# Low halves of the routed tokens: made by GpSimd from SBUF instead of by VectorE from PSUM

## What is computed

```python
x = x + hierarchical_moe(rms_norm(x, ffn_norm[l]), ...)      # 4 groups x 8 experts, top 2 of one group
# inside, per token:
pg = softmax(xt @ w_rg + b_rg);  g_w, g_idx = top_k(pg, 1)
le = (xt @ w_re + b_re)[g_idx];  tv, tj = top_k(le, 2)
w_top = softmax(tv) * g_w
# tokens are gathered for each expert, then
gu = xb @ w_e1[e];  ys = (silu(gu[:, :512]) * gu[:, 512:]) @ w_e2[e]
y[token] += ys * w_top
```

## Time and profile before

| | us |
|---|---|
| median of 3 runs | 1590.48 (1589.98 to 1591.97) |
| the profiled execution | 1589.14 |
| its span, first to last instruction | 1587.3 |

### The profile page before, as it was taken

One profiled execution on the slowest core, in us unless ns is written; L12 is line 12 of the kernel. 1 busy time (PEld: TensorE's weight loads), 2 busy tenths in 40 slices (PEclk: granted clock), 3 DMA queues, 4 the chain that ended last, 5 costly groups with the idle time before them and its releaser, 6 DMA issues.

```text
span 1587.3 us, 31259 instructions
## 1 busy us (share of the span) xinstructions
PE 1314.4 (83%) x13623; PEld 1020.7 (64%) x13623; DVE 598.0 (38%) x987; ACT 447.4 (28%) x665; POOL 0.4 (0%) x5
## 2 busy tenths in 40 slices
PE   9999999998777586877679999999986656767755
PEld 8999999995354263544448999999754323324422
DVE  5869647644121101212118885566431101101101
ACT  7544545532120110102016454554301001000101
POOL 0000000000000000000000000000000000000000
PEclk9999999999889788999979999999999988878988
DMA  9843458449999999999997544664799999999996
GB/s 356 294 162 107 160 188 315 147 169 392 416 427 420 427 426 422 427 420 426 427 387 233 198 149 160 242 251 148 281 417 429 425 428 424 427 428 414 427 427 281
DMA packets 93839, 520.02 MB, mean 328 GB/s; under 512 B 9850, under 2 KB 17410, under 8 KB 68356
## 3 DMA queue, kind: packets, MB, share of 16 engines
q1 hardware_dynamic: 92956, 515.94, 81.1%
q10 hardware_dynamic: 744, 2.05, 0.4%
HBM read 515.87 MB, written 2.10 MB: 326 GB/s over the span
## 4 chain that ended last, share of the span: by engine, by line
PE 53%; DMA 36%; DVE 6%; ACT 2%; issue 2%; SPq 2%; DVEq 0%; ACTq 0%
DMA ring<-in_w_expert_out 29%; PE banks L1759 29%; PE banks L2202 6%; PE banks L2155 5%; DMA ring<-in_w_expert_in 4%; PE banks L1790 4%; PE banks L2216 2%; DMA ring<-in_w_in 2%; PE banks L2172 2%; DVE w_lo L1066 1%; DVE stat L1520 1%; PE banks L1988 1%; SPq L514 1%; ACT w_hi L647 1%; DMA lnt<-in_positions 1%
## 5 line engine op out<-in xcount | busy, mean ns | idle before, releaser
L2155 PE MATMUL banks<-ring,arena 128*32 128x256 f32 x3904 | 267.1, 423 | 123.0 <-DMA ring<-in_w_expert_in 117.3
L2155 PEld LDWEIGHTS banks<-ring,arena 128*32 128x32 f32 x3904 | 125.9, 119 | 247.3 <-DMA ring<-in_w_expert_in 147.4
L1066 DVE TENSOR_TENSOR w_lo<-ring,w_hi 128x2048 fp32r<-128x2048 f32 (+1 forms) x103 | 210.5, 2044 | 108.9 <-ACTq L624 97.1
L1759 PE MATMUL banks<-h_hi,w_hi 128*128 128x256 f32 x776 | 221.8, 286 | 0.9 <-DVEq L1057 0.9
L2202 PE MATMUL banks<-ring,arena 128*32 128x256 f32 x2048 | 154.2, 451 | 81.8 <-DMA ring<-in_w_expert_out 68.6
L1759 PE MATMUL banks<-h_hi,w_lo 128*128 128x256 f32 x776 | 219.5, 283 | 0.0
L1002 ACT ACTIVATE arena<-banks 128x128 f32<-128x128 f32 x66 | 18.4, 278 | 689.1 <-PE banks L2155 689.1
L1513 DVE TENSOR_TENSOR arena<-arena,banks 128x128 f32<-128x128 f32 x66 | 19.1, 289 | 504.2 <-ACT arena L1002 504.2
L1759 PE MATMUL banks<-h_lo,w_hi 128*128 128x256 f32 x712 | 201.4, 283 | 0.0
L647 ACT CAST w_hi<-ring 128x2048 fp32r<-128x2048 f32 (+1 forms) x103 | 176.1, 1709 | 70.0 <-PE banks L1759 43.0
L2202 PEld LDWEIGHTS banks<-ring,arena 128*32 128x32 f32 x2048 | 76.2, 125 | 137.4 <-issue 79.4
(11 more groups left out here) (434 smaller groups left out, 2179.9 us busy)
## 6 DMA issues: line engine op xcount, KB each, us to landing
ring<-in_w_expert_in SPq DMA_DIRECT2D x120, 2048.0 KB, 23.3
ring<-in_w_expert_out SPq DMA_DIRECT2D x60, 2048.0 KB, 24.1
ring<-in_w_in SPq DMA_DIRECT2D x23, 2048.0 KB, 9.2
ring<-in_w_branch SPq DMA_DIRECT2D x12, 1024.0 KB, 5.2
ring<-in_w_out SPq DMA_DIRECT2D x4, 2048.0 KB, 7.9
ring<-in_w_xq SPq DMA_DIRECT2D x4, 2048.0 KB, 7.9
ring<-in_w_xo SPq DMA_DIRECT2D x4, 2048.0 KB, 8.4
arena<-in_w_xkv SPq DMA_DIRECT2D x4, 2048.0 KB, 21.3
```

Of the source, the lines that this page charges most:

```text
L1066: post(dve.tensor_tensor(piece_view(w_lo, *key), piece_view(ring, *key), high_view(*key).bitcast(F32), ALU.subtract), "w_split")
L1759: ins = pe.matmul(acc, stationary(a, k), moving(b, k), start=k == 0 and n == 0, stop=k == kc - 1 and n == 2)
L2155: ins = pe.matmul(G[32 * j:32 * j + 32, :], tokens, w[:, k % 4, :, j * P:(j + 1) * P], start=k == 0, stop=k == KC - 1, tile_position=(0, 3 ...
```

## The change

ScalarE now does two instructions for each job j, not one, from the same bank with the same scale: `htok_hi` rounded, and `htok_full` in plain f32. They no longer wait for completion one by one; ScalarE waits once for all eight and then frees the four banks itself. GpSimd, in a queue of its own, waits for both of job j (`htok_high` counts eight per layer) and subtracts, four instructions of 128x512 per layer, both operands in SBUF. `htok_full` is `region(0, TB, D)`, the words 0 to 2047 of `arena`, so the subtraction works in place: `htok_lo` lies over the same words. `token_low` goes from VectorE, with the wait for its end and the freeing of the banks. TensorE's steps r = 0 and 1 wait for two of GpSimd's four subtractions, r = 2 and 3 for all four.

```diff
+        htok_full = region(0, TB, D)
...
         def _(pool):
             pool.memset(ones[:, :], 1.0).then_inc(S["pool_step"], 1)
+            for layer in range(L):
+                for j in range(4):
+                    half, tb = j // 2, j % 2
+                    part = lambda v: v[:, tb, half * 512:half * 512 + 512]
+                    pool.wait_ge(S["htok_high"], 8 * layer + 2 * j + 2)
+                    pool.tensor_tensor(part(htok_lo), part(htok_full), part(htok_hi).bitcast(F32), ALU.subtract).then_inc(S["htok_ready"], 1)
...
                     acc = job_wait(act, layer, "htok", j)
-                    post(act.activation(htok_hi[:, tb, half * 512:half * 512 + 512].rearrange("t (k p) -> t k p", k=4),
-                                        acc.rearrange("t (p k) -> t k p", k=4), ACT.Copy, scale=rstd_tok[:, tb:tb + 1]), "htok_high")
+                    for v in (htok_hi, htok_full):
+                        act.activation(v[:, tb, half * 512:half * 512 + 512].rearrange("t (k p) -> t k p", k=4),
+                                       acc.rearrange("t (p k) -> t k p", k=4), ACT.Copy, scale=rstd_tok[:, tb:tb + 1]).then_inc(S["htok_high"], 1)
+                act.wait_ge(S["htok_high"], 8 * (layer + 1))
+                for j in range(4):
+                    act.sem_inc(free(layer, "htok", j), 1)
...
-                def token_low(r):
-
-                    half, pair = r // 2, r % 2
-                    part = lambda v, tb: v[:, tb, r * T:(r + 1) * T].rearrange("t (k p) -> t k p", k=2)
-                    for tb in range(TB):
-                        dve.wait_ge(S["htok_high"], 4 * layer + 2 * half + tb + 1)
-                        acc = job_wait(dve, layer, "htok", 2 * half + tb).rearrange("t (p k) -> t k p", k=4)
-                        dve.scalar_tensor_tensor(part(htok_lo, tb), acc[:, 2 * pair:2 * pair + 2, :], rstd_tok[:, tb:tb + 1],
-                                                 part(htok_hi, tb).bitcast(F32), ALU.mult, ALU.subtract).then_inc(S["htok_ready"], 1)
...
                 def weights():
-                    for r in range(4):
-                        token_low(r)
-                    dve.wait_ge(S["htok_ready"], 8 * (layer + 1))
-                    for j in range(4):
-                        dve.sem_inc(free(layer, "htok", j), 1)
                     dve.sem_inc(free(layer, "place"), 1)
...
                         if small_jobs:
-                            pe.wait_ge(S["htok_ready"], 8 * layer + 2 * r + 2)
+                            pe.wait_ge(S["htok_ready"], 4 * layer + 2 * (r // 2) + 2)
```

## The result

The changed kernel took 1603.52 us (median of 6 runs, 1599.37 to 1604.37) against 1590.23 us before (6 runs, 1589.56 to 1591.97): ratio 1.0077, 95% interval 1.0067 to 1.0088, so it is 0.8% slower, 12 to 13 us. The forecast was 1602.8 us, slower. The profiled execution took 1599.37 us, the lowest of the six (the next is 1602.38), with a span of 1597.2 us; what it shows is about 4 us less than what the median has.

The account below looks back on a forecast made before the run. TensorE held 53% of the chain that ended last, DMA 36%; delay before the gather's release counts in full. Per layer -0.17 + 4.12 + 2.2 = 6.15 us, twice 12.3, made the median 1602.8 us; range 1590 to 1607.

Parts of the forecast that it names:

- Where the stage stands: Stretch from TensorE's filling to the experts' first ring load: every microsecond of delay before the gather's release counts in full.
- VectorE: Per layer, removing token_low's eight instructions (3.22 us) saves only TensorE's wait for its first pair: -0.17 us.
- ScalarE: Eight instructions per layer, 0.63 us apart, finish before the first gather is done: 0 us, with 0.3 kept as possible.
- GpSimd's own time: Four 128x512 subtractions per layer at 1.2 us each, ending at 361.5 if undisturbed, in time for TensorE.
- limit of 3.3 us for one subtraction: Up to this length per GpSimd subtraction, TensorE's wait for the new low halves was to cost nothing.
- rival of a late GpSimd: GpSimd starts late or one subtraction takes over 3.3 us: +6 to +10 us per layer, 1602 to 1610; chance 0.06.
- The hold: GpSimd's subtractions delay VectorE's serial router chain by full exclusion: mask 4.12 us late per layer, at 364.47.
- The rule: Two-SBUF-input VectorE instructions and SBUF-reading GpSimd instructions share one read interface; the second waits for the whole first: 4.12 us.
- The clock: After 5.0 us idle before `place`, TensorE runs at half clock: 2.2 us per layer, ends 0 and 2.5.
- The sum: Per layer -0.17 + 4.12 + 2.2 = 6.15 us, twice 12.3, giving a median of 1602.8 us.
- rival of no disturbance: VectorE's chain keeps its 0.25 us steps while GpSimd subtracts: 1590.1 us, or 1590.7 with ScalarE's 0.3; chance 0.22.
- the one with the clock up: GpSimd's subtractions delay VectorE's chain but TensorE's clock holds: +7.9 us, 1598.4 us; chance 0.19.

## Why the prediction was right

- *Where the stage stands.* The delay in front of the first ring load went to the end in full, but for 1.45 us of 11.35 (the 0.25, 0.25 and 0.95 of above), which are no larger than the runs of one kernel differ.
- *VectorE*: put at -0.17 us. The wait for `htok_lo` is gone, and in the run with more filling, where the clock stays up, the gather starts 369.34 - 367.01 = 2.33 us after `place`, not 2.85; at the ring load 0.39 us of this is left. So the term was too small by 0.2 us. Freeing 3.2 us of VectorE gave no more than that.
- *ScalarE*: free, as put. Eight instructions every 0.57 us, where 0.63 was taken.
- *GpSimd's own time*: 1.23 us for a subtraction, where 1.2 was taken from VectorE's row of twice the columns. That it came so near is in part luck: GpSimd's only row, 0.205 us for 128 columns, would make 2.5 us for three passes over 512 columns, not 1.0 to 1.4. The Trainium skill's figure (GPSIMD Engine Reference, § Performance versus the Vector engine), scaled, gave an estimate of 1.12, a tenth too low here. The subtractions were ready in time (361.1, needed at 363 and later). The forecast's limit of 3.3 us for one subtraction holds for the first two only; all four by 366.5 from 356.5 on allows 2.5 us. At 1.23 us neither mattered, and the rival of a late GpSimd is out.
- *The hold*: 4.12 us in the sum, 3.70 measured. The step was right and its walk off in one place: I let the TENSOR_SCALAR L1462 (L1473 after) pass as a one-operand instruction. It was held, 1.20 us, and one two-operand instruction fewer instead. What made the sum smaller is when the row of subtractions ended: 361.13, not 361.93, because ScalarE delivered faster and GpSimd went from one to the next without letting VectorE in between; the instruction held behind one subtraction ended within 0.1 us of its end, when the next had begun. In these traces VectorE gets one such instruction for each subtraction, and a hold for each: four for four, two for two.
- *The rule*: the Trainium skill (SBUF — State Buffer, § Who interferes with whom) has this, and the runs agree: GpSimd's reading holds VectorE's two-operand instructions (copies, subtractions), its writing alone does not (memsets), reductions pass in 0.22 us, and TENSOR_SCALAR is named there as one that can take the shared pair in a two-port mode, which is the sentence I had not applied (1.20 us beside a subtraction, and the lengthened 0.23 us beside a memset would fit it too). The runs show one direction only. That GpSimd waits for VectorE in turn was in my walk, but no trace here shows it: all subtractions from two tiles took 1262 to 1281 ns.
- *The clock*: 2.2 us per layer in the sum, with an end of 2.5. Measured 2 to 3 by the times, with 3.2 (2.1 to 4.3) where it is measured by itself, and 2.7 in that run's trace. The end of 2.5 was too low: the changed kernel's layer 0 lost 3.07 us, with the clock at half from before 364 to past 370, six to seven us and not 4.9.
- *The sum*: 12.3 us forecast, 12 to 13 measured. Per layer the hold was 0.42 us smaller and VectorE's gain 0.2 larger than put, and the clock some 0.5 dearer (2.7, not 2.2). These nearly cancel, so the total is better than its terms, and that is luck; the mechanism is not.

The rival of no disturbance is refuted by VectorE's rows, and the one with the clock up describes, within a microsecond, the run with more filling: 1598.4 forecast for it, 1597.66 measured. None of these versions was faster than the kernel before beyond the noise; the nearest, with ScalarE's part alone, has a ratio of 0.9995 (0.9986 to 1.0005). The changed kernel gives up 3.7 us of a serial chain to take 3.2 us off an engine that nobody was waiting for.

What stays open: why the changed kernel's runs spread more (1599.4 to 1604.4) than those of before (1589.6 to 1592.0). With more filling they spread less, 1596.8 to 1599.7, and in the profiled run layer 0 lost 6.39 us and layer 1 4.96 with equal holds. The difference lies in how long the granted clock was below 1.00: from 363 to 371 in layer 0, from 1145 to 1149 in layer 1. That points to the clock, but no run was made for it.

## What to carry to other kernels

An elementwise operation given to GpSimd is not free because GpSimd is idle: look at what VectorE does at that very time. If it is a serial chain of small two-operand instructions on the path to the end, each GpSimd instruction that reads SBUF can stretch one of them to nearly its own length, as here one of 0.17 us to 1.10. Look for the loss in the length of the instructions, not in waits. And where filling products keep TensorE's clock up, a wait that becomes a few microseconds longer can cost twice unless the filling grows with it: here 3.7 us of idle time cost another 1.7 to 3.1 us at half clock.

## What the runs showed of the hardware that I had not expected

- A TENSOR_SCALAR of 128x8 with one SBUF operand was held by a GpSimd subtraction for 1.20 us in place of 0.17, while a TENSOR_REDUCE passed in 0.22 us and a RECIPROCAL in 0.17.
- GpSimd's subtraction of 128x512 took 1.04 us with the same tile as both operands and an f32 output (four in 4.03 us), and 1.27 us, one every 1.23, with two tiles and an `fp32r` output. Which of the two differences makes it was not tried.
- GpSimd's copy of 128x512 took 0.62 us, and its memset 0.52; with a wait after each, eight memsets took 4.60 us.
- The granted clock fell to 0.50 after an idle time of only 2.47 us in both layers (two subtractions alone), and after 2.13 us in one layer of two (copies). In these three cases it fell only 1 to 2 us after TensorE had resumed: at 364.3 after 363.23, at 1142.5 after 1140.56, at 1140.1 after 1138.16.
